# Dense projections in three token groups (512, 512, 256) per weight tile instead of four of 320

## What is computed

```
h = rmsnorm(x);  z = h @ w_in            # w_in: 1024 x 9216
u, v, q, i, z_f, z_b, g_o, g_a, g_b = split(z)
ya = gelu(u) * (w_s[g] @ rmsnorm(gelu(v)) + b_s)      # gMLP: 8 groups, chunks of 128 tokens
yb = rmsnorm(gla(q, i, z_f, z_b)) * silu(g_o)         # 8 heads, 128 x 128 state, both directions
m  = sigmoid(g_a) * (ya @ w_branch_a) + sigmoid(g_b) * (yb @ w_branch_b)
x  = x + m @ w_out
x  = x + 16 SwiGLU experts, each on its top 2*T/16 tokens of each sequence
y  = rmsnorm(x)
```

## Time and profile before

| what | value |
|---|---|
| median of 3 runs | 2849.87 us |
| the profiled execution | 2844.18 us |
| its span, first to last instruction | 2842.4 us, mean TensorE clock 0.958 |
| TensorE matmuls busy | 2596.3 us (91%) in 18702 matmuls |
| VectorE, ScalarE, GpSimd busy | 1519.1 (53%), 962.7 (34%), 670.5 us (24%) |

### The profile page before, as it was taken

The page is one execution under the profiler, slowest core; times in us unless marked ns, Lnnn a source line. Parts: engine busy times, 40 slices in busy tenths (PEclk is TensorE's granted clock), DMA queues, the critical chain, the costliest instruction groups (busy, mean ns, idle before and its releaser), DMA issues. The chain is left out here.

```text
span 2842.4 us, 49715 instructions
## 1 busy us (share of the span) xinstructions
PE 2596.3 (91%) x18702; PEld 2548.4 (90%) x18702; DVE 1519.1 (53%) x2298; ACT 962.7 (34%) x1569; POOL 670.5 (24%) x502
## 2 busy tenths in 40 slices
PE   5999899999999999999859997955999999999993
PEld 4999799999999999999859997935999999999993
DVE  4123300035755755755631112156889889889894
ACT  4222311122122122122121102142665665655653
POOL 1321311133523523523522113112010010010110
PEclk7999999999999999999879997976999999999997
DMA  3112321210110100110023215064788788788774
GB/s 112 30 36 89 127 72 48 65 38 16 47 31 15 46 31 15 46 31 15 17 92 99 90 61 193 15 251 148 255 264 278 255 264 277 246 275 270 253 243 165
DMA packets 332493, 349.58 MB, mean 123 GB/s; under 512 B 12048, under 2 KB 309008, under 8 KB 332432
## 3 DMA queue, kind: packets, MB, share of 16 engines
q1 hardware_dynamic: 326288, 327.79, 34.7%
q0 software_dynamic: 6144, 20.98, 3.5%
HBM read 301.54 MB, written 47.19 MB: 123 GB/s over the span
## 5 line engine op out<-in xcount | busy, mean ns | idle before, releaser
L1772 PE MATMUL ex_out<-ex_xT,ex_w_hi 128*128 128x320 f32 x2048 | 533.0, 347 | 2.3 <-DVE ex_xT L1610 2.3
L1773 PE MATMUL ex_out<-ex_xT,ex_w_lo 128*128 128x160 f32 x2048 | 484.0, 236 | 0.0
L1592 DVE TENSOR_TENSOR ex_w_lo<-ex_raw,ex_w_hi 128x1024 fp32r<-128x1024 f32 x374 | 455.0, 1217 | 0.4
L1586 ACT ACTIVATE ex_w_hi<-ex_raw 128x1024 fp32r<-128x1024 f32 x384 | 387.2, 1045 | 26.8 <-PE ex_out L1773 13.9
L1773 PEld LDWEIGHTS ex_out<-ex_xT,ex_w_lo 128*128 128x128 f32 x2048 | 392.6, 192 | 0.0
L1772 PEld LDWEIGHTS ex_out<-ex_xT,ex_w_hi 128*128 128x128 f32 x2048 | 385.8, 188 | 2.9 <-DVE ex_xT L1610 2.4
L1772 PE MATMUL ex_out<-ex_hT,ex_w_hi 128*128 128x320 f32 x1024 | 279.1, 351 | 0.2
L174 PE MATMUL hg_proj<-trunk_h_hi,hg_w_hi 128*128 128x320 f32 x768 | 244.6, 318 | 0.0
L1773 PE MATMUL ex_out<-ex_hT,ex_w_lo 128*128 128x160 f32 x1024 | 241.8, 236 | 0.0
L175 PE MATMUL hg_proj<-trunk_h_lo,hg_w_hi 128*128 128x320 f32 x768 | 237.4, 309 | 0.0
L176 PE MATMUL hg_proj<-trunk_h_hi,hg_w_lo 128*128 128x320 f32 x768 | 237.4, 309 | 0.0
(11 more groups left out here) (318 smaller groups left out, 6226.9 us busy)
## 6 DMA issues: line engine op xcount, KB each, us to landing
ex_raw<-in_w_exp_gate_dram SPq DMA_DIRECT2D x64, 1024.0 KB, 4.9
ex_raw<-in_w_exp_up_dram SPq DMA_DIRECT2D x64, 1024.0 KB, 4.9
ex_raw<-in_w_exp_down_dram SPq DMA_DIRECT2D x64, 1024.0 KB, 5.5
trunk_w_raw<-in_w_in_dram SPq DMA_DIRECT2D x48, 512.0 KB, 4.2
hg_w_raw<-in_w_in_dram SPq DMA_DIRECT2D x16, 512.0 KB, 3.9
ya<-gm_ya SPq DMA_DIRECT2D x8, 640.0 KB, 3.4
m_a<-ma_m SPq DMA_DIRECT2D x8, 640.0 KB, 3.4
yb<-hg_Kt_b SPq DMA_DIRECT2D x8, 640.0 KB, 5.1
```

The source lines that it names most:

```text
L1586: nc.scalar.activation(w_hi[t % RING][:], raw[p % RAW][:, :, c:c + P], ACT.Copy).then_inc(s["w_hi_ready"], 1)
L1592: ops.tensor_tensor(w_lo[t % RING][:], raw[p % RAW][:, :, c:c + P], w_hi[t % RING][:].bitcast(F32), ALU.subtract).then_inc(lo_done(e, t)[0 ...
L1772: nc.tensor.matmul(bank[:, 0:2 * SLOTS], w_hi[i][:, k, :], B[:, k, :], start=(k == 0), stop=False)
L1773: mm = nc.tensor.matmul(bank[:, SLOTS:2 * SLOTS], w_lo[i][:, k, :], B[:, k, 0:SLOTS], start=False, stop=(k == KC - 1))
```

## The change

A tile's 1280 tokens are taken in three groups of 512, 512 and 256 columns. Since a tile now has an odd number of groups, the count of groups that each bank has served is worked out by `on_bank` and `freed`. In `hgrn2` a round has 15 groups, and the last of one round and the first of the next use the same bank 0. Its steps follow the first 12 groups: steps 0 to 7 after groups 0 to 7, with step 8 (KTF) right behind step 7, and steps 9 to 12 after groups 8 to 11. GpSimd has three levels behind each weight split. The parts after which `gmlp` and `residual` transpose and mix keep their numbers, so the mix (part 2) now follows the tile's last group. In the first round of a merge, BRANCH part 0 waits for the first half of the rows and parts 1 and 2 for all; the gate parts are moved after pieces 3, 8 and 14 (before: 2, 6, 10 and 14).

```diff
-PART = 320
-PARTS = T // PART
+PART_COLS = (slice(0, 512), slice(512, 1024), slice(1024, T))
+PARTS = len(PART_COLS)
...
+        self.per_round = [self.on_bank(b, PARTS * per) for b in range(2)]
+    def on_bank(self, b, groups):
+        return (groups + 1 - b) // 2
+    def freed(self, b, r, groups):
+        return self.per_round[b] * r + self.on_bank(b, groups) + CREDIT
...
-        pe.wait_ge(self.bank_free[b], PARTS // 2 * self.per * r + g // 2 + CREDIT)
-        out, c = self.out[b][:, 0:PART], slice(part * PART, (part + 1) * PART)
+        pe.wait_ge(self.bank_free[b], self.freed(b, r, g))
+        out, c = self.bank(part, b), PART_COLS[part]
...
-            eng.wait_ge(self.bank_free[b], PARTS // 2 * (self.per * r + t + 1) + CREDIT)
+            eng.wait_ge(self.bank_free[b], self.freed(b, r, PARTS * (t + 1)))
...
+        def steps_after(n):
+            if n == KTF - 1:
+                return (n, KTF)
+            return [step for step in (n if n < KTF else n + 1,) if step < STEPS]
...
-                if g is not None and n < STEPS:
-                    pe_step(pe, g, n)
+                if g is not None:
+                    for step in steps_after(n):
+                        pe_step(pe, g, step)
...
-                    act_gla(act, g, n)
+                    for step in steps_after(n):
+                        act_gla(act, g, step)
...
-                    if j == PARTS:
+                    if j == 4:
                         dve_output_gate(dve, g)
...
-                            rows.ready(pe, KC * (1 + 2 * part // PARTS))
+                            rows.ready(pe, KC if PART_COLS[part].stop <= T // 2 else 2 * KC)
```

More of the change, by code:

```diff
@@ L182, in result, with bank @@
         eng.wait_ge(self.group_done, PARTS * self.per * r + g + 1 + PARTS * CREDIT)
-        return self.out[g % 2][:, 0:PART], self.bank_free[g % 2]
+        return self.bank(part, g % 2), self.bank_free[g % 2]
+    def bank(self, part, b):
+        c = PART_COLS[part]
+        return self.out[b][:, 0:c.stop - c.start]
     def moved(self, eng, r, t):
         for b in range(2):
-            eng.wait_ge(self.bank_free[b], PARTS // 2 * (self.per * r + t + 1) + CREDIT)
+            eng.wait_ge(self.bank_free[b], self.freed(b, r, PARTS * (t + 1)))
     def pe_credit(self, pe):
@@ L504, in act_move @@
             out, free = W.result(act, r, t, part)
-            c = slice(part * PART, (part + 1) * PART)
+            c = PART_COLS[part]
             if t == TI:
@@ L523, in dve_project @@
                 lb, om = C.lb[:, z, bass.ds(r, 1)], C.one_minus_lb[:, z, bass.ds(r, 1)]
-                for b in range(2):
-                    dve.wait_ge(W.bank_free[b], PARTS // 2 * (W.per * r + t + 1) + CREDIT)
+                W.moved(dve, r, t)
                 nc.vector.tensor_scalar(f[:], f[:], om, lb, ALU.mult, ALU.add).then_inc(s["gates_ready"], 1)
@@ L538, in pe_values @@
         def pe_values(pe, r):
-            for b in range(2):
-                pe.wait_ge(W.bank_free[b], PARTS // 2 * (W.per * r + TI + 1) + CREDIT)
+            W.moved(pe, r, TI)
             pe.wait_ge(s["y_ready"], NY * r + CREDIT)
@@ L703, in dve_start @@
             dve.wait_ge(s["gates_ready"], 6 * (g + 1))
-            for b in range(2):
-                dve.wait_ge(W.bank_free[b], PARTS // 2 * (W.per * g + TQ + 1) + CREDIT)
+            W.moved(dve, g, TQ)
             dve.wait_ge(s["gla_step"], gla_at(g - 1, OUT))
@@ L902, in act_move @@
                 out, free = W.result(act, r, t, part)
-                nc.scalar.activation(act_out[t][:, part * PART:(part + 1) * PART], out,
+                nc.scalar.activation(act_out[t][:, PART_COLS[part]], out,
                                      ACT.Gelu_apprx_tanh).then_inc(free, 1)
@@ L1144, in act_gate @@
             out, free = W.result(act, r, GATE, part)
-            nc.scalar.activation(sg[:, part * PART:(part + 1) * PART], out, ACT.Sigmoid).then_inc(free, 1)
+            nc.scalar.activation(sg[:, PART_COLS[part]], out, ACT.Sigmoid).then_inc(free, 1)
         def act_round(act, r, last):
@@ L1164, in dve_round @@
                 if adds:
-                    W_done = PARTS // 2 * (PER * r + BRANCH) + part // 2 + 1 + CREDIT
-                    dve.wait_ge(W.bank_free[(PARTS * BRANCH + part) % 2], W_done)
+                    done = PARTS * BRANCH + part
+                    dve.wait_ge(W.bank_free[done % 2], W.freed(done % 2, r, done + 1))
                     nc.vector.tensor_tensor(m[:, c], m[:, c], m_prev[:, c], ALU.add).then_inc(s["added"], 1)
@@ L1276, in act_round @@
                     out, free = W.result(act, r, t, part)
-                    nc.scalar.activation(o[t][:, part * PART:(part + 1) * PART], out, ACT.Copy).then_inc(free, 1)
+                    nc.scalar.activation(o[t][:, PART_COLS[part]], out, ACT.Copy).then_inc(free, 1)
         with st.block() as block:
```

## The result

The changed kernel takes 2866.1 us (median of 5, 2862.6 to 2867.9) against 2849.7 for the kernel before (5 runs beside it, 2846.0 to 2851.6). The ratio is 1.0062 with a 95% interval of 1.0051 to 1.0073: slower by 16.5 us, where 2828 was forecast. The profiled execution has a span of 2864.3 us, 21.9 more than the 2842.4 of before; it is 5 us more than the medians differ by, since the profiled execution of before, 2844.2 us, lies that much under its median. Ratios and their intervals are of fast executions alone; medians are of all, with one slow execution (2971.2 us at a granted clock of 0.829) among the four of the fourth experiment.

The account below looks back on a forecast made before the run. Up to the router TensorE's own queue was taken as the bound. gMLP -5, merges -4, recurrence -10 and output -2.5 made -22 us: 2822 on the profiled 2844.2, 2828 as a median; range 2806 to 2848.

Parts of the forecast that it names:

- the gMLP's first half, tiles alone: gMLP V half: only the cheaper matmuls of its tiles were counted, -0.5 us, with no new wait.
- the recurrence: Recurrence: shorter waits -8.6, 40 cheaper tiles -2.8, less cover in the last round +1.2, together -10 us.
- the price of a matmul: All 96 retiled tiles: 24 fewer matmuls a tile at 3 ns each save 0.07 us a tile, 7 us in all.
- almost all per column: TensorE matmuls: price 0.44 to 0.456 ns a column, with only 1 to 6 ns left per matmul, taken as 3.
- The 3.9 us wait: gMLP, first U tile: TensorE's third group waits for ScalarE; some 0.8 us would be left, gain about 5 us.
- The first round of the second merge: Second merge, first round: 8.4 us left after the last lo piece in place of 10.6, estimated at -2 us.
- The waits that I removed: Recurrence: OUT's 0.63 us a round and 0.3 each at levels 5 and 6 go, -8.6 us over 7 rounds.
- KTF behind step 7: Recurrence: KTF right behind step 7 causes no wait; its keys are ready 5.5 us after step 6, it comes 8 after.
- 1.5 to spare: Recurrence, step 2: GpSimd's level 1 ends at 39.1 us after OUT's end, step 2 is due at 40.6, no wait.
- the slower rival: Recurrence, between ONES and step 2: VectorE and GpSimd become the round's bound, 8 us a round, 2870 us; chance 0.09.
- The last round: Recurrence, last round: two groups of cover in place of three, costing +1.2 us.
- my -2.5: Output projection: -1.9 us for part 0's wait for rows and -0.6 for cheaper tiles, -2.5 us together.

Follow-up runs that it names:

- the fourth experiment: Groups of 512, 512 and 256 in both merges and the output projection alone, gMLP and recurrence as in the kernel before: 2834.4 us, ratio to it 0.9948.
- two cures: Changed kernel with the V tile's turn behind the next tile's first group, 2827.6 us; or with GpSimd's weight split ahead of the square, 2828.5 us.
- the late turn alone: Kernel before, four groups of 320, with only the turn of a V tile moved one group later, behind the third: 2878.0 us, ratio 1.0104.
- the first and the fourth experiment: First: changed kernel, turn of a V tile behind the next tile's first group, not second: 2827.6 us. The fourth experiment has its own line.
- the kernel with level 1 first: Changed kernel with GpSimd's level 1 of K ahead of the query tile's weight split in each recurrence round: 2866.4 us, ratio 1.0070.
- the order changed as well: Changed kernel with earlier V turn, shorter forward gate tile wait, level 1 ahead of the split, and output gate tile as 512, 256, 512: 2810.6 us.

## Why the prediction was wrong, point by point

The step that turned the sign is the term of the gMLP's first half, tiles alone (-0.5), with the wait for GpSimd's weight split put at nothing: it measured +33.4. Two more terms failed, the recurrence (-10, measured +3.8) and the price of a matmul (7 us on 96 tiles, measured 29), and they pull in opposite directions.

- **Price of a matmul.** The step that failed is "almost all per column". I took the slope between two durations, 236 ns at 160 and 309 at 320, for the slope of the price, and subtracted a tail found on plain fp32. A duration is not a pitch, and the 160-column row belongs to a stream that sits on the floor of 0.11 us. Pitches at 320, 512 and 256 columns show N / 2.4 + 13 to 14 ns. Error: 22 us, on the cautious side. What the Trainium skill (TensorE: Matmul & The Clock Gate, Back-to-back issue gap) gives for a single gap, N / 2.4 + 2.5 ns, has the right form and a constant five times too small for this mode; its 131 ns for a stream at N = 512 is 96 ns under the trace.
- **gMLP, V half.** The failure that turned the sign: +33.4 us where the sum had -0.5. The forecast asked of each wait in the list what becomes of it, and of the recurrence's queues what stands behind what, but not of a stage that showed no wait. `part == 1` was unchanged text whose meaning moved from 640 to 1024 columns. The rows for it were in the trace before: the split ends 0.2 us ahead of its use. My only remark on it was that the chain before the first U tile "is 0.6 later". By the forecast's own price, 5.59 us for a group of 512, the turn comes 11.2 us into its tile and not 7.0, 4 us later, against 0.2 us of slack; that was there to be worked out. Three experiments show this cause: each of two cures takes the whole loss away, and the late turn alone brings it into the kernel before.
- **gMLP, U half.** Right in sum, -4.8 against -4.5. The 3.9 us wait is gone. The first U tile took 17.7 us in place of 22.2, though its first group ran at a lower clock behind the last of the V half's waits. The last mix cost 1.3 us where I had 1.1: from the end of TensorE's last matmul to the next stage's first it is now 8.77 us and was 7.51. The tiles between gave 0.25 each, by the price.
- **Merges.** The 13 tiles between the first round and the last tile gave 0.30 each in both, 3.8 to 3.9 us a merge. The first round of the second merge took 40.8 us in place of 43.4, 2.6 less (I had 2 beside the tiles' price); in the profiled executions of the first and the fourth experiment it took 41.5 and 39.5. In the first merge the first round took 3.3 us longer where I had none: BRANCH part 1 needs all rows, waits 5.5 us for the last lo pieces, and runs at a lower clock behind it. No run takes that wait away by itself.
- **Recurrence.** The waits that I removed went (OUT, levels 5 and 6: 1.5 us a round). Two gaps that I had at nothing ate them. One is the third group of the forward gate tile, 1.7 us a round: for KTF behind step 7 I had asked only whether its keys are ready, not who waits for KTF, and had not looked that up in `act_buffers`. The other is step 2, 1.5 us a round, where I had 1.5 to spare: the slower rival had the place and the mechanism, and its size, 8, was wrong. I had the copy of level 1 end 33.5 us after OUT's end and it came at 34.3; GpSimd's level 1 ended at 40.6 and not 39.1, 0.3 us after TensorE was through with the group in front. Later still was the one link that I had at its undisturbed price, VectorE's products of level 1, beside that level: 3.8 us in place of 1.6. The last round, from the first matmul of its only tile to the next stage's, took 97.7 us in place of 91.1: 6.6 more, not 1.2. It has one level more without a group in front, and TensorE waits for Q products six times there, 13.2 us in all, where it waited 7.9 in four. No run here isolates this. The four tiles ahead of the first round and that round gave 1.2 and 1.5 us; with the 6.6 these make the +3.8.
- **Output.** The -3.4 to the end of the run is near my -2.5 by luck. The stage itself gave 4.4: eight tiles at 0.30 are 2.4 (I had 0.6), which leaves 2.0 for the wait (I had 1.9). Unchanged code behind it took 1.0 more.
- **The range.** It reached up to 2848 by adding small losses, and its slower rival lay in the recurrence. No case held a new wait in a stage without one. One sum was also off: the slower rival turns the sign from 43.7 us on (3.1 us in each of 7 rounds is 22), and 44.5 is where it would be 5 us slower than before.

## What to carry to other kernels

When the size of a piece of work changes, look for every instruction placed by counting pieces, and follow what is queued behind it on the other engines to where it is next needed; the slack there is the number to compare, and where it is near zero there is no wait in the profile to warn you. A wait of a few microseconds on TensorE can cost its own length and, behind it, a stretch at the lower clock: here 3.7 and then 1.7 us. When two engines hold a step together, removing either cause alone shows nothing; that is no proof that the cause is not real.

## What the runs showed of the hardware

- With every group 128 or 160 columns wide, TensorE's records follow each other almost without a gap (808.5 of 809 us, 548.8 of 551), and the granted clock is 0.50 (1.2 GHz) all the way; it does not rise in the stage. With 512-column groups between them, matmuls of 128 columns run at 1.0. The same matmul costs 0.213 or 0.112 us. So these two stages, cut into narrow matmuls throughout, cost twice what the floor says. Each was seen in one execution.
- The shared cost of VectorE and GpSimd moves with the queue: in three kernels a weight split of GpSimd's stretched, by its place, the gates' scaling (2.96 for 0.94), the second Q product (3.65 for 1.48) or the product of level 1 (3.01 for 0.82). The Trainium skill (SBUF — State Buffer, Who interferes with whom) calls the shared pair an exclusive lock; the traces agree: in the kernel with level 1 first, the product issued at 985.30 us ends 0.7 us after the split beside it does (987.63), as if it had stood until then. Moving that split alone brought nothing (107.0 us a round); only with the order changed as well did it pay, at 104.36.
